# Which engine splits four weight slabs, and when the sparse rows are worked on, in a one-core attention and PEER block

## The reference

```python
x = x + ga1 * (merged @ w_out)                      # conv and attention mixers, gated
h2 = rms_norm(x, norm2_g) * (1 + sc2) + sh2
x = x + ga2 * peer_ffn(h2, peer_wq, peer_keys, peer_u, peer_v)
```

```python
q = (ht @ peer_wq).reshape(T, 8, 2, 128)            # 8 heads
s = einsum('thpd,hpkd->thpk', q, peer_keys)         # 128 scores for each half key
sv, si = top_k(s, 16); cand = sv[..., 0, :, None] + sv[..., 1, None, :]
top, pos = top_k(cand, 16)                          # 16 experts of each head: 128 picks a token
g = softmax(top)
a = gelu(einsum('td,thkd->thk', h, peer_u[ib]))     # ib: numbers of the picked experts
out = einsum('thk,thkd->td', g * a, peer_v[ib])
```

## Time and profile before

| | us |
|---|---|
| median of 3 runs | 1592.05 (1588.79 to 1592.96) |
| the profiled execution, its own time | 1593.64 |
| its span | 1591.8 |
| PE busy | 1553.2 (98%) |
| DVE busy | 1355.9 (85%) |
| ACT busy | 631.5 (40%) |
| POOL busy | 593.5 (37%) |
| bytes moved by DMA | 442.38 MB, mean 278 GB/s |

### The profile page before, as it was taken

The page is one execution under the profiler, slowest core; times in us unless marked ns, Lnnn a source line. Parts: engine busy times, 40 slices in busy tenths (PEclk is TensorE's granted clock), DMA queues, the critical chain, the costliest instruction groups (busy, mean ns, idle before and its releaser), DMA issues.

```text
span 1591.8 us, 23427 instructions
## 1 busy us (share of the span) xinstructions
PE 1553.2 (98%) x8490; PEld 1348.1 (85%) x8490; DVE 1355.9 (85%) x2600; ACT 631.5 (40%) x972; POOL 593.5 (37%) x421
## 2 busy tenths in 40 slices
PE   8999999999999999989999999999999999999998
PEld 4777678887889999988999888888888888888887
DVE  6899787765699889998985798899888998998886
ACT  4433835235334344434443333333333333333332
POOL 0000100102435624465403355565455555555540
PEclk9999999999999999999999999999999999999999
DMA  8421255654424669998889999999999999999992
GB/s 333 154 100 41 77 193 171 236 188 146 151 88 124 194 231 311 353 305 252 252 283 365 403 371 376 378 380 397 377 370 381 379 388 390 377 382 373 376 376 95
DMA packets 195277, 442.38 MB, mean 278 GB/s; under 512 B 57761, under 2 KB 100961, under 8 KB 195042
## 3 DMA queue, kind: packets, MB, share of 16 engines
q1 hardware_dynamic: 130480, 248.97, 43.7%
q0 software_dynamic: 52880, 175.73, 30.1%
q10 hardware_dynamic: 11810, 16.27, 2.9%
HBM read 395.75 MB, written 45.11 MB: 277 GB/s over the span
## 4 chain that ended last, share of the span: by engine, by line
PE 74%; DVE 14%; DMA 6%; issue 2%; ACT 2%; SPq 1%; DVEq 0%; ACTq 0%
PE bank L1767 13%; PE bank L1768 12%; PE bank L1769 12%; PE bank L2118 10%; PE bank L2119 10%; PE bank L2120 10%; DVE sb_w_lo L1125 3%; DMA sb_stage<-v_dram 3%; DVE sb_spare L1636 2%; DVE sb_x L1586 2%; PE bank L2097 1%; PE bank L2023 1%; DMA sb_stage<-u_dram 1%; DVE sb_x L1582 1%; ACT sb_w_hi L772 1%
## 5 line engine op out<-in xcount | busy, mean ns | idle before, releaser
L772 ACT ACTIVATE sb_w_hi<-sb_stage 128x1024 fp32r<-128x1024 f32 x324 | 343.0, 1060 | 463.3 <-PE bank L2120 242.7
L1767 PE MATMUL bank<-sb_act_hi,sb_w_hi 128*128 128x352 f32 (+1 forms) x1408 | 488.4, 347 | 2.9 <-DVE sb_w_lo L1125 2.2
L1768 PE MATMUL bank<-sb_act_lo,sb_w_hi 128*128 128x352 f32 (+1 forms) x1408 | 482.3, 343 | 0.0
L1769 PE MATMUL bank<-sb_act_hi,sb_w_lo 128*128 128x352 f32 (+1 forms) x1408 | 481.9, 342 | 0.0
L1125 DVE TENSOR_TENSOR sb_w_lo<-sb_stage,sb_w_hi 128x1024 fp32r<-128x1024 f32 x290 | 354.3, 1223 | 103.4 <-ACT sb_w_hi L772 100.8
L2118 PE MATMUL bank<-sb_w_hi,sb_mix_hi 128*128 128x512 f32 x768 | 300.4, 391 | 6.4 <-DVE sb_mix_lo L1625 6.4
L2119 PE MATMUL bank<-sb_w_lo,sb_mix_hi 128*128 128x512 f32 x768 | 299.9, 390 | 0.0
L2120 PE MATMUL bank<-sb_w_hi,sb_mix_lo 128*128 128x512 f32 x768 | 299.3, 390 | 0.0
L1767 PEld LDWEIGHTS bank<-sb_act_hi,sb_w_hi 128*128 128x128 f32 x1408 | 265.4, 189 | 22.8 <-issue 4.4
L1768 PEld LDWEIGHTS bank<-sb_act_lo,sb_w_hi 128*128 128x128 f32 x1408 | 265.6, 189 | 16.5 <-issue 0.5
L1769 PEld LDWEIGHTS bank<-sb_act_hi,sb_w_lo 128*128 128x128 f32 x1408 | 265.4, 188 | 15.1
(11 more groups left out here) (265 smaller groups left out, 1971.0 us busy)
## 6 DMA issues: line engine op xcount, KB each, us to landing
sb_stage<-u_dram SPq DMA_DIRECT2D x128, 512.0 KB
sb_stage<-v_dram SPq DMA_DIRECT2D x128, 512.0 KB
sb_stage<-w_front_dram SPq DMA_DIRECT2D x68, 512.0 KB
sb_scr<-w_ada_dram POOLq DMA_DIRECT2D x32, 512.0 KB, 4.4
a_scratch<-sb_scr ACTq DMA_DIRECT2D x80, 192.0 KB
sb_scr<-a_scratch SPq DMA_DIRECT2D x16, 960.0 KB
g_old_scratch<-sb_scr SPq DMA_DIRECT2D x11, 1280.0 KB
sb_scr<-g_old_scratch SPq DMA_DIRECT2D x16, 880.0 KB
```

The source lines that it names most:

```text
L772: nc.scalar.activation(w_hi[:, slot, :], stage[:, slot, :], ACT.Copy).then_inc(w_round, 1)
L1767: nc.tensor.matmul(out, w_hi[:, slot, w], rhs_hi[:, dc, :], start=(i == 0), stop=False)
L1768: nc.tensor.matmul(out, w_hi[:, slot, w], rhs_lo[:, dc, :], start=False, stop=False)
L1769: last = nc.tensor.matmul(out, w_lo[:, slot, w], rhs_hi[:, dc, :], start=False, stop=(i == len(dcs) - 1))
```

## The change

It moves work and adds one wait; no instruction's size is changed.

- `POOL_SLABS` goes from 20 to 16: POOL's last low half is that of slab 15, and DVE makes those of slabs 16 to 19 too. The four splits inside the first list are now those of slabs 16 to 19, and six bare splits follow it in place of two.
- The first list is turned behind slab 20 (was 22), and the exponentials come at slab 17 (was 20).
- The first 16 sparse dots begin one step earlier and are spread over 14 steps (were 12); the second 16 begin at step 21 (was 14) and are spread over 17 (were 12). Steps are counted from slab 24.
- Each early dot comes one step later, the last two together.
- POOL's fifth row for the laps waits until DVE has made the first product (`c_mul`).

```diff
-S_FIRST = (2, 14)
-S_UNITS = 12
+S_FIRST = (1, 21)
+S_UNITS = (14, 17)
-EXP_SLAB = 20
-POOL_SLABS = 20
-LIST_SLAB = 22
+EXP_SLAB = 17
+POOL_SLABS = 16
+LIST_SLAB = 20
...
-    return [S_HALF * half + d for d in range(S_HALF) if 0 <= k == d * S_UNITS // S_HALF]
+    return [S_HALF * half + d for d in range(S_HALF) if 0 <= k == d * S_UNITS[half] // S_HALF]
...
                             elif n == 1:
                                 pool.wait_ge(row_used, EARLY_DOTS)
+                            elif n == 4:
+                                pool.wait_ge(c_mul, 1)
...
-                        if it * G_UNITS + b == S_FIRST[half] + S_UNITS + 1:
+                        if it * G_UNITS + b == S_FIRST[half] + S_UNITS[half] + 1:
                             sparse_weights(half)
...
-            for n in (4, 5):
+            for n in range(4, 10):
                 split_unit(POOL_LAST + n, (POOL_LAST + n) % RING)
...
             for b in range(EARLY - G_LAST):
                 split_unit(FRONT + G_LAST + b + 2, (FRONT + G_LAST + b + 2) % RING)
-                if b < EARLY_DOTS:
-                    early_dot(b)
+                if b >= 1:
+                    early_dot(b - 1)
+            early_dot(EARLY_DOTS - 1)
             nc.vector.memset(acc, 0.0).then_inc(acc_zero, 1)
```

More of the change, by code:

```diff
@@ L152 @@
 DOT_LAPS = LAPS - AHEAD_LAPS
-assert TURN_TOKENS == P and G_FIRST + 2 == POOL_SLABS + 6
+assert TURN_TOKENS == P and G_FIRST + 2 == POOL_SLABS + 10
 EARLY_ROWS = (1, 2, 3)
@@ L1028, in g_turn @@
                     for half in range(2):
-                        if it * G_UNITS + b == S_FIRST[half] + S_UNITS:
+                        if it * G_UNITS + b == S_FIRST[half] + S_UNITS[half]:
                             act.wait_ge(s_used, S_HALF * (half + 1))
@@ L1667, in _ @@
                 split_unit(FRONT + G_LAST + b + 2, (FRONT + G_LAST + b + 2) % RING)
-                if b < EARLY_DOTS:
-                    early_dot(b)
+                if b >= 1:
+                    early_dot(b - 1)
+            assert EARLY - G_LAST == EARLY_DOTS
+            early_dot(EARLY_DOTS - 1)
             nc.vector.memset(acc, 0.0).then_inc(acc_zero, 1)
```

## The result

| | kernel before | changed kernel |
|---|---|---|
| median of 20 runs, us | 1591.12 (1588.79 to 1595.41) | 1594.09 (1591.77 to 1597.61) |
| ratio, with its 95% interval | | 1.0020 (1.0014 to 1.0026) |
| the profiled execution, its own time | 1593.64 | 1593.63 |
| its span | 1591.8 | 1591.4 |

The change makes the kernel slower by 3.2 us (2.2 to 4.1). The time lies in the stated range and 0.2% above the 1591.4 that I said, but the forecast of -0.7 has the wrong sign.

The account below looks back on a forecast made before the run. PE, busy 98% of the span, was taken as the bound, with data bounding the laps' start. A 3.0, B -5.7 and C 2.0 summed to -0.7, taking the median 1592.05 to 1591.4 us; range 1586 to 1598.

Parts of the forecast that it names:

- C: Slab 72 into the laps: later adds delay early rows, which compete with a `v_dram` slab; costs 2.0 us (-4.7 to 7.7).
- hidden, by 0.6 us: Slabs 76 and 77: DVE's splits behind early dots are done by 853.9, so PE does not wait for them.
- 872 is still early enough: Laps' start: first product at 872, not 870.12, costs nothing, since ACT stood until 873.49 for a `v_dram` slab.
- A: First list: four low halves move from POOL to DVE; PE waits 1.3 and 1.7 us near slabs 18, 19; costs 3.0.
- B: Turns two and three: later sparse dots cut PE's loss from 10.9 to 5.2 us, one slow step included; gives 5.7 back.
- The reading of one copy in the earlier trace: DVE's ranking before slab 16: without POOL's low half, a 1.57 us copy saves 1.4 to 1.5; ranking done at 549.1.
- The same instructions in another place, priced at nothing: First list: earlier exponentials and earlier turning of the list cost nothing; a PE wait would be under 3.80 us.
- The balance of DVE's work against PE's steps: Steps 18 to 37: DVE's work 107.4 us, PE's 100.6; deficit 6.8, lead 3.0, leaving 3.8 as PE waits.
- (2): Early rows: POOL's tail decides, rows land late and the product passes 873.5; +5, 1597; chance 0.21.
- (1): Turn three: DVE has enough room, B's waits nearly vanish and C stays hidden; -6, 1586; chance 0.26.
- (3): Slabs 18, 19 and turn three: two slow clock steps make +2.8, 1594; chance 0.53 shared with forecast and (4).
- (4): Whole kernel: the edits do nothing, bytes and PE's work being the same; 1592; chance 0.53 shared with forecast and (3).

Follow-up runs that it names:

- kernel 3: Changed kernel without the second 16 sparse adds, gate tiles waiting for the first 16 alone: -3.0 us (-4.3 to -1.6) against before.
- kernel 5: As kernel 3, with POOL's early rows also held until about 836 us: +2.1 us (0.6 to 3.5) against before.
- kernel 13: Kernel before with ACT's first rounding of the product moved ahead of a v_dram slab's rounding: -0.2 us (-1.6 to 1.4) against before.
- kernel 14: Changed kernel with the same other order on ACT as kernel 13: +3.7 us (2.2 to 5.1) against before.
- kernel 2: Changed kernel with part A undone (POOL's low halves, exponentials and first list as before): +2.4 us (0.6 to 4.1) against before.
- kernel 6: Kernel before with only the second 16 sparse dots moved, to steps 20 to 33: -5.1 us (-6.8 to -3.3) against before.
- kernel 8: As kernel 6, with each early dot one step later, the last two together: -4.9 us (-6.8 to -3.0) against before.
- kernel 7: Kernel before with only the second 16 sparse dots moved, to steps 17 to 30: -1.9 us (-3.3 to -0.5) against before.
- kernel 10: As kernel 8, with the first 16 sparse dots one to a step: -7.6 us (-9.5 to -5.7) against before.

## Why the prediction was wrong

**The sign came from one term: C, 2.0 predicted, 5.2 measured.** The step that failed is the sentence "three rows of 512 KB at 387 GB/s are 4.1 us of all DMA engines; about half of that stands ahead of the slab". The mechanism was there, with its lateness (the first early row 5.4 us behind the start of slab 72 predicted, 841.6 against 836.2, and 5.7 measured, 837.90 against 832.17), and only half its price was taken. Kernels 3 and 5 measure the late rows at 5.1 (3.1 to 7.1), which leaves out the half. Kernels 13 and 14 make it likely why halving was wrong: a wait that is taken away at the first `peer_v` slab comes back eight slabs later, so what does not stand ahead of this slab stands ahead of another that PE waits for. With 4.1 the forecast would have been +1.4, and with the measured 5.2 it is +2.5. The rule of the Trainium skill that I weighed there ("DMA: Bandwidth & Descriptors", section "Issuing engines are not separate DMA queues": all issuers share the same 16 DMA engines) gave 4.1; the 5.1 of kernels 3 and 5 agrees with it and not with my half, though late dots can have a part in it.

**A second error in C: "hidden, by 0.6 us" and "872 is still early enough".** The sum set new times for rows and product against before's times for PE, though A and B together were to bring PE there 2.7 us earlier. Slab 80 began at 864.61, 3.7 earlier than before (1.6 of it lay ahead of slab 16), and the first product, at 871.35, came 6.7 behind it, where 3.7 was predicted. Each early dot waits for a row, and behind it stand the split, then the load that needs the slot. I had checked only whether PE wanted the slab. POOL issued the first two at 837.90 and 839.19, and their dots began at 846.08 and 849.17, 8.2 and 10.0 us later (I took 7.7). DVE stood still for the first of them:

```profile
846.08 1.23 DVE L1595 CUSTOM_DVE_ANT_0 sb_wide<-sb_wide,sb_htok 128x1024 f32<-128x1024 f32 x1 [10.50 <-DMA sb_wide<-u_rows_dram,sb_scr]
```

PE hardly felt it, +0.4 in slabs 72 to 79. But the chain above runs through such a dot to SP's load and the tiles behind it.

**A, 3.0 predicted, 3.3 measured in the profile and 3.8 (2.4 to 5.3) alone.** The reading of one copy in the earlier trace rows held. In the changed kernel's timeline of DVE its like takes 0.17, and the first split starts 1.9 us behind it, after the rest of ranking and a cast of 0.22:

```profile
545.93 0.17 DVE L1465 COPY sb_small<-sb_wide 128x8 f32<-128x8 f32 x1
...
547.82 1.22 DVE L1127 TENSOR_TENSOR sb_w_lo<-sb_stage,sb_w_hi 128x1024 fp32r<-128x1024 f32 x1
```

With the 1.56 us between the executions, ranking ended at 549.1 to 549.2 in before's time, as computed. The two waits were 1.40 and 1.34 (1.3 and 1.7 predicted). What I missed is that A also brings the sparse rows ten microseconds earlier, without which the first dots' earlier step would cost 3.8 (kernel 2, in its profiled execution). "The same instructions in another place, priced at nothing" overlooked who was waiting for them.

**B, -5.7 predicted, -5.5 measured.** Turn two lost 1.3 in place of 10.9, turn three 4.1 in place of 0; I had 5.2 for both, and they are 5.4, the slow step included. The balance of DVE's work against PE's steps is what carried this. But the gain was not worth its number, since the same late dots that made it also moved POOL's adds behind the last list. In kernels 6 and 8 turns two and three are 6.0 and 6.2 us shorter than before, and nothing is lost at the rows; kernel 7 gains 0.5 there.

**The rivals.** (2), POOL's tail, is what happened, though not where I put it. Its point of decision was a first row later than 849.9, with PE's slab 72 at 836.2, thus 13.7 us behind it. By the clock it was not reached (846.08); against PE, whose slab 72 began at 832.17, it was just reached, with 13.9. But PE waited only 0.1 us in slabs 72 to 79, so it was not one late split that cost the time. It ended at +3.2 where I had priced it at +5, had a chance of 0.21, and with C's full share the forecast would have gone its way. (1) falls: neither did B's waits vanish nor did C stay hidden. (3), the clock, adds nothing to the sum: no slow step follows the waits near slabs 18 and 19 (granted clock 1.00 from 550.94 to 585.68), turn two's mean clock rose to 1.00, and turn three's fell to 0.98, the one slow step that B already held. Its reading that only a wait of 2.7 brings a slow step was wrong: in before, PE waited 2.24 ahead of 693.60, and the step from 694.49 took 6.36 us at 0.73 as well. (4) is excluded by the interval. The new wait on `c_mul` costs and saves nothing, as assumed.

## What to carry to other kernels

When an engine that issues transfers is made late, count the bytes that leave a stretch with spare DMA time and enter a full one, and charge all of them to the full stretch, divided by its rate. Here that count gives 4.1 us, and 5.1 (3.1 to 7.1) were measured for all that the late rows did. Spread work only as far as its last consumer has slack. Here the whole gain of spreading the dots was kept with the last one three steps earlier, where POOL's adds end 3 to 5 us behind the list that its next gathers need (kernels 6, 8 and 10). And where two profiled executions are compared, compare stages by their own lengths: these two were equally long, and the kernels differ by 3.2 us in their medians.

## What the runs showed of the hardware

- SP's issue of one DMA mostly took 0.33 us, but up to 8.45 in a stretch with the DMA engines full (share 1.04). The last of the gate tiles' DMAs held SP for 8.45 us in the changed kernel and 4.14 before, and the `v_dram` load behind it was issued only then. It held it for 7.15 in kernel 3 too, which loses nothing there, so this alone does not make the difference. The timelines of before and of the changed kernel:

```profile
859.11 4.14 SPq L589 DMA_DIRECT2D sb_scr<-g_sparse_scratch  x1
```

```profile
857.01 8.45 SPq L589 DMA_DIRECT2D sb_scr<-g_sparse_scratch  x1
```

- A gathered row of 512 KB, put at 7.7 us, took 9.96 in the chain of the changed kernel and 11.81 in that of kernel 5, and a slab load in the full stretch up to 20.62 (kernel 13).
- Taking away a wait did not take away the slow step: in kernel 13 PE ran through the laps' start without one and had it eight slabs later, at a mean clock of 0.81 and 0.73 in the two steps around the wait of 5.8.
